# Half of the down products in the summed quarters by seven block products, in equal super-units

## What is computed

```python
x = x + cross_attention(rms_norm(x, g_cross[l]), mem_n, w_cq[l], w_ckv[l], w_co[l])
u = jnp.einsum('bsd,df->bsf', rms_norm(x, g_mlp[l]), w_up[l])
x = x + jnp.einsum('bsf,fd->bsd', jnp.square(jax.nn.relu(u)), w_down[l])
```

## Time and profile before

| what | us |
|---|---|
| median of 3 runs (1203.5 to 1203.62) | 1203.58 |
| the profiled execution's own time | 1203.42 |
| its span | 1201.6 |
| TensorE busy | 1182.1 |
| VectorE busy | 853.1 |
| ScalarE busy | 628.7 |
| POOL busy | 177.8 |

### The profile page before, as it was taken

The page is one execution under the profiler, slowest core; times in us unless marked ns, Lnnn a source line. Parts: engine busy times, 40 slices in busy tenths (PEclk is TensorE's granted clock), DMA queues, the critical chain, the costliest instruction groups (busy, mean ns, idle before and its releaser), DMA issues.

```text
span 1201.6 us, 19272 instructions
## 1 busy us (share of the span) xinstructions
PE 1182.1 (98%) x6776; PEld 1035.6 (86%) x6776; DVE 853.1 (71%) x1149; ACT 628.7 (52%) x927; POOL 177.8 (15%) x177
## 2 busy tenths in 40 slices
PE   9999999999999999999999999999999999999996
PEld 7888899999989889888788888788888888888885
DVE  5758766786668867676887666877767787666554
ACT  6445455555645657555544555544655454555442
POOL 2907400030322404200000000000000000000341
PEclk9999999999999999999999999999999999999999
DMA  9674553443644543456456454547543746555531
GB/s 357 252 260 173 196 175 140 162 154 140 246 162 165 181 159 142 151 198 209 166 176 253 175 181 168 210 149 271 175 176 139 264 157 220 191 182 187 198 140 70
DMA packets 51455, 224.43 MB, mean 187 GB/s; under 512 B 3792, under 2 KB 4176, under 8 KB 31696
## 3 DMA queue, kind: packets, MB, share of 16 engines
q1 hardware_dynamic: 50688, 220.22, 50.8%
q10 hardware_dynamic: 720, 3.59, 0.8%
HBM read 221.69 MB, written 2.10 MB: 186 GB/s over the span
## 4 chain that ended last, share of the span: by engine, by line
PE 93%; DVE 3%; ACT 1%; issue 1%; POOL 1%; DMA 1%; SPq 0%; DVEq 0%; ACTq 0%; POOLq 0%
PE bank L1301 16%; PE bank L1298 16%; PE bank L1299 15%; PE extra L1557 6%; PE extra L1559 5%; PE extra L1558 5%; PE bank L1303 4%; PE bank L1305 4%; PE bank L1304 4%; PE bank L1344 3%; PE bank L1346 3%; PE bank L1345 3%; DVE w_low L813 1%; PE bank L1570 1%; PE bank L1571 1%
## 5 line engine op out<-in xcount | busy, mean ns | idle before, releaser
L813 DVE TENSOR_TENSOR w_low<-staged,w_high 128x1024 fp32r<-128x1024 f32 x311 | 390.0, 1269 | 145.5 <-ACT w_high L433 134.9
L433 ACT ACTIVATE w_high<-staged 128x1024 fp32r<-128x1024 f32 x304 | 314.6, 1053 | 189.8 <-PE bank L1301 81.2
L1299 PEld LDWEIGHTS bank<-part_a,w_low 128*128 128x128 f32 x1408 | 264.6, 188 | 61.4
L1298 PE MATMUL bank<-part_a,w_high 128*128 128x512 f32 x704 | 281.0, 399 | 0.0
L1301 PE MATMUL bank<-part_a,w_high 128*128 128x512 f32 x704 | 278.5, 396 | 0.0
L1299 PE MATMUL bank<-part_a,w_low 128*128 128x256 f32 x1408 | 276.8, 278 | 0.0
L719 ACT ACTIVATE w_high<-staged 128x1024 fp32r<-128x1024 f32 x114 | 118.9, 1058 | 108.9 <-PE extra L1559 92.0
L1133 DVE TENSOR_TENSOR w_low<-staged,w_high 128x1024 fp32r<-128x1024 f32 x114 | 137.4, 1221 | 33.8 <-ACT w_high L719 32.6
L361 POOL TENSOR_TENSOR squares<-x 128x256 f32<-128x256 f32 (+1 forms) x31 | 37.3, 1204 | 685.2 <-DVE x L1257 661.3
L1298 PEld LDWEIGHTS bank<-part_a,w_high 128*128 128x128 f32 x704 | 133.7, 190 | 0.6 <-DVE w_low L813 0.3
L1301 PEld LDWEIGHTS bank<-part_a,w_high 128*128 128x128 f32 x704 | 132.0, 187 | 0.0
(11 more groups left out here) (201 smaller groups left out, 1775.1 us busy)
## 6 DMA issues: line engine op xcount, KB each, us to landing
staged<-in_wup SPq DMA_DIRECT2D x64, 1024.0 KB, 4.8
staged<-in_wdown SPq DMA_DIRECT2D x64, 1024.0 KB, 5.0
staged<-in_wqk SPq DMA_DIRECT2D x32, 1024.0 KB, 4.8
staged<-in_wv SPq DMA_DIRECT2D x12, 1024.0 KB, 5.4
staged<-in_wbc SPq DMA_DIRECT2D x8, 1024.0 KB, 4.8
staged<-in_wmk SPq DMA_DIRECT2D x4, 1024.0 KB, 4.7
staged<-in_woa SPq DMA_DIRECT2D x4, 1024.0 KB, 4.8
staged<-in_wcq SPq DMA_DIRECT2D x4, 1024.0 KB, 4.8
```

The source lines that it names most:

```text
L433: nc.scalar.activation(w_high[:, job % 2, cols], staged[:, job % 4, cols], ACT.Copy).then_inc(high_ready, 1)
L813: tt(w_low[:, job % 2, cols], staged[:, job % 4, cols], f32(w_high[:, job % 2, cols]), ALU.subtract).then_inc(low_ready, 1)
L1298: mm(out[:, :], high, both, start=first, stop=False)
L1299: last = mm(out[:, 0:T], low, part[:, slot(kt), 0, :], start=False, stop=False)
```

## The change

A summed quarter's down product is now four super-units (pairs) of equal form. Pairs 0 and 1 belong to the first 1024 outputs, 2 and 3 to the others. A pair takes one unit by seven products (0 or 2) and one ordinary unit (1 or 3): 42 + 48 matmuls in 11 halves, in the order of three products, half of the ordinary unit, four products, the other half. The products' weights always use slots 0 and 1, the ordinary unit's always 2 and 3. The seven products' sums stay in PSUM over two pairs, and only then four sums of 128x1024 add them to running sums, which are kept apart per PSUM bank in a `y` of twice the size. They are combined once, by twelve VectorE sums in the first eight up jobs of quarter 3; the transposes follow, four behind each of the last eight up jobs. The token sums are made for units 0 and 2, in the first and the third up group. Before the first pair, the split of its first ordinary half comes ahead of the last up tile's arithmetic. The two norm sums move into the first half of the second job. The wait for the cleared `y` moves to the first pair. PSUM is named as two tensors of four banks, and `rope` moves into space that is used again later.

```diff
 SUMMED_QUARTERS = 3
-GROUP_HALVES = 20
-GROUP_STEPS = 12
-QUARTER_HALVES = 2 * QUARTER + 2 * GROUP_HALVES
-FREE_STEPS = 8
-H_SUMS, H_B, H_C = 7, 12, 16
+PAIRS = 4
+PAIR_HALVES = 12
+GROUP_STEPS = 4
+QUARTER_HALVES = 2 * QUARTER + PAIRS * PAIR_HALVES
+FREE_STEPS = 4
+H_B11, H_B21, H_B22, H_R, H_T, H_R_END = 0, 1, 2, 3, 5, 10
+SLOT_S, SLOT_R = 0, 2
...
-        part_s = sb("part_s", [P, 2, 2, 4 * P], F32R)
-        common = sb("common", [P, 2, 512])
+        part_s = sb("part_s", [P, 4, 2, 4 * P], F32R)
+        y_right = sb("y_right", [P, 8, 512])
...
+                    for s, free in enumerate((-2, -2, H_T - PAIR_HALVES, 0)):
+                        sp.wait_ge(low_ready, mlp(q)(2) + (H_MLP + free))
+                        sp.dma_start(staged[:, s, :], wup_in[q * 16 + s, :, :]).then_inc(landed[s], 16)
...
+            def load_down(q):
+                for k in range(PAIRS):
+                    load_unit(q, k, k % 2 * 2, SLOT_S, (-2, -2) if k else (-6, -4))
+                    load_unit(q, k, k % 2 * 2 + 1, SLOT_R, (H_T - PAIR_HALVES, 0) if k else (-2, 0))
...
+            nc.gpsimd.memset(y[0], 0.0).then_inc(y_clear, 1)
+            nc.gpsimd.memset(y[1], 0.0).then_inc(y_clear, 1)
...
             with act.Fori(0, SUMMED_QUARTERS) as q:
-                up_group(q, 0, True)
-                with act.Fori(1, QUARTER // 4 - 1) as i:
-                    up_group(q, i)
+                up_group(q, 0, 0)
+                up_group(q, 1)
+                up_group(q, 2, 2)
                 for s in range(4):
                     if s < 2:
                         split(mlp(q, 3), JOB_MLP + s + 2, 0)
-                    else:
-                        s_tiles(q, 0, (2 * s - 4,))
-                    up(q, 3, s)
-                    if s < 2:
+                        up(q, 3, s)
                         split(mlp(q, 3), JOB_MLP + s + 2, 1)
                     elif s == 2:
-                        s_tiles(q, 0, (1,))
+                        s_tile(q, 0, H_B11)
+                        up(q, 3, s)
+                        s_tile(q, 0, H_B21)
                     else:
-                        r_tiles(q, 0, 3, SLOT_RA[0], 0, (0,))
-                for g in range(2):
-                    r_tiles(q, g, 3, SLOT_RA[g], 2 * g, (1, 2, 3))
-                    s_sums(q, g)
-                    r_tiles(q, g, H_B, SLOT_RB[g], 1 + g, (0, 1, 2, 3)) if g == 0 else r_tiles(
-                        q, g, H_B, SLOT_RB[g], 3, (0, 1, 2, 3))
-                    r_tiles(q, g, H_C, SLOT_RC[g], 1 + 2 * g, (0, 1, 2, 3))
-                    if g == 0:
-                        s_tiles(q, 1, (0, 1, 2))
-                        r_tiles(q, 1, 3, SLOT_RA[1], 2, (0,))
+                        s_tile(q, 0, H_B22)
+                        r_tile(q, 0, 0)
+                        up(q, 3, s)
+                for k in range(PAIRS):
+                    r_tile(q, k, 1)
+                    s_sums(q, k)
+                    r_tile(q, k, 2)
+                    r_tile(q, k, 3)
+                    if k < PAIRS - 1:
+                        for n in (H_B11, H_B21, H_B22):
+                            s_tile(q, k + 1, n)
+                        r_tile(q, k + 1, 0)
...
+            def step(q, k, n):
+                pair = (banks_all, extras_all)[n // 2][:, n % 2 * 2:n % 2 * 2 + 2, :]
+                to = y[k // 2][:, 2 * n:2 * n + 2, :]
+                dve.wait_ge(half_done, down_half(q, k) + (H_T + 1, H_T + 3, H_R_END, PAIR_HALVES)[n])
+                tt(to, to, pair, ALU.add).then_inc(y_step, 1)
+
+            def down_pair(q, k, ahead):
+
+                last = k % 2
+                sum_of_weights(q, k, 1)
+                r_tile(q, k, 1)
+                sum_of_weights(q, k, 2)
+                s_sum(q, k, 0)
+                sum_of_weights(q, k, 3)
+                for n in range(1, 4):
+                    s_sum(q, k, n)
+                r_tile(q, k, 2)
+                if last:
+                    step(q, k, 0)
+                r_tile(q, k, 3)
+                if last:
+                    step(q, k, 1)
                 ahead(0)
+                if last:
+                    step(q, k, 2)
                 ahead(1)
-                step(q, g, 8)
-                step(q, g, 9)
                 ahead(2)
-                step(q, g, 10)
-                step(q, g, 11)
+                if last:
+                    step(q, k, 3)
                 ahead(3)
...
+            def combine(g, n):
...
+                to, one, two = ((y[g][:, 4, :], y[g][:, 4, :], m1), (m6, m6, m1), (m7, m7, m6),
+                                (y[g][:, 6, :], y[g][:, 6, :], m6), (tokens_2, tokens_2, twice(3)),
+                                (right, right, twice(1)))[n]
...
+                tt(to, one, two, ALU.add).then_inc(y_made, 1)
...
+                        r_tile(q, 0, 0)
+                        up(q, 3, s)
+                dve.wait_ge(y_clear, 2)
+                for k in range(PAIRS):
+                    down_pair(q, k, next_pair(q, k + 1) if k < PAIRS - 1 else next_quarter(q))
...
+                    if between is not None and n == count // 2:
+                        norm_sum(between, extra[3])
...
+            def down_pair(q, k):
+                unit, opens, ends = k % 2 * 2, k % 2 == 0, k % 2 == 1
+                steps = q * (2 * GROUP_STEPS) + (FREE_STEPS + k // 2 * GROUP_STEPS)
+                if k == 0:
                     pe.wait_ge(taken, mlp(q)(1) + (BANKS + OUT_MLP + 13))
-                pe.wait_ge(hid_low, q * 16 + (1 + 4))
-                pe.wait_ge(y_step, steps - 4)
-                s_half(q, g, 0, bank[0], block_of(0, 0), ends=True)
-                pe.wait_ge(y_step, steps - 3)
-                s_half(q, g, 1, extra[0], block_of(1, 0))
-                pe.wait_ge(y_step, steps - 1)
-                pe.wait_ge(s_low, q * 2 + 2)
-                s_half(q, g, 2, extra[1], sum_of(3))
-                pe.wait_ge(y_step, steps)
-                for n in range(4):
-                    r_half(q, g, 3, n, 1)
-                if g == 0:
+                pe.wait_ge(hid_low, q * 16 + (1 + 4 * unit + 4))
+                if opens:
+                    pe.wait_ge(y_step, steps - 3)
+                s_half(q, k, H_B11, bank[0], block_of(unit, 0, 0), opens, ends)
+                if opens:
+                    pe.wait_ge(y_step, steps - 1)
+                s_half(q, k, H_B21, extra[0], block_of(unit, 1, 0), opens)
+                if opens:
+                    pe.wait_ge(y_step, steps)
+                pe.wait_ge(s_low, q * 4 + (unit + 2))
+                s_half(q, k, H_B22, extra[2], sum_of(unit, 3), opens)
+                r_half(q, k, 0)
+                r_half(q, k, 1)
+                if k == 0:
                     pe.wait_ge(taken, mlp(q)(1) + (BANKS + OUT_MLP + 16))
-                s_half(q, g, H_SUMS, bank[1], sum_of(0), ends=True)
-                s_half(q, g, H_SUMS + 1, bank[3], sum_of(2), ends=True)
-                s_half(q, g, H_SUMS + 2, bank[2], sum_of(1), ends=True)
-                s_half(q, g, H_SUMS + 3, extra[2], block_of(1, 1), opens=False, done_by=2)
-                for n in range(4):
-                    r_half(q, g, H_B, n, 2)
-                for n in range(4):
-                    r_half(q, g, H_C, n, 3)
+                s_half(q, k, H_T, bank[1], sum_of(unit, 0), opens, ends)
+                s_half(q, k, H_T + 1, bank[3], sum_of(unit, 2), opens, ends)
+                s_half(q, k, H_T + 2, bank[2], sum_of(unit, 1), opens, ends)
+                s_half(q, k, H_T + 3, extra[1], block_of(unit, 1, 1), ends=ends, done_by=2)
+                r_half(q, k, 2)
+                r_half(q, k, 3)
...
+            for n in range(KT // 2):
                 up(3, n // 4, n % 4)
-                if n == 0:
-                    pe.wait_ge(y_step, SUMMED_QUARTERS * 2 * GROUP_STEPS + FREE_STEPS)
+            for n in range(KT // 2):
+                up(3, 2 + n // 4, n % 4)
+                g = n // 4
+                if n % 4 == 0:
+                    pe.wait_ge(y_made, 6 * g + 6)
                 if n >= 4:
                     pe.wait_ge(y_added, n - 3)
-                for t in range(QT):
-                    last = nc.tensor.transpose(extra[n % 4][:, t * P:(t + 1) * P],
-                                               y[:, t, n * P:(n + 1) * P], ident)
+                for tile in range(2 * n, 2 * n + 2):
+                    for t in range(QT):
+                        last = nc.tensor.transpose(
+                            extra[n % 4][:, tile % 2 * T + t * P:tile % 2 * T + (t + 1) * P],
+                            y[g][:, 4 + 2 * (tile % 8 // 4) + t, tile % 4 * P:(tile % 4 + 1) * P], ident)
                 last.then_inc(y_turned, 1)
```

More of the change, by code:

```diff
@@ L307, in _, with load_up @@
             stream(wco_in, JOB_CO, CROSS)
-            def load_up(q):
-                with sp.Fori(0, QUARTER // 4) as i:
+            def load_up(q, first):
+                if first:
+                    for s in range(4):
```

(36 more changed lines are left out.)

293 lines of the change are left out of this document (121 added, 172 removed).

## The result

The changed kernel takes 1213.26 us (median of 4 runs, 1212.03 to 1213.92), the kernel before 1203.54 in the same comparison: a ratio of 1.0078, 95% interval 1.0064 to 1.0093. It is slower by 9.7 us. Forecast were 1210.0, within 1198 to 1215; the measured time lies 3.3 us above the first and 0.3 above the likeliest case's own range (1206 to 1213). The profiled execution took 1212.03 us with a span of 1210.2.

What follows compares the result with a forecast made beforehand. TensorE, busy 98% of the span, was taken to bound the kernel, with VectorE and the load queue next. 1203.4 - 8.2 - 3.3 - 2.0 - 0.6 + 20.7 = 1210.0 us, range 1198 to 1215.

Steps and rivals of the forecast that it cites:

- likeliest case: Whole kernel: gets slower, products saved on TensorE being paid by VectorE and loads released late; 1206 to 1213 us, chance 0.48.
- TensorE's work: Down stage: 186 matmuls per group become 180, so 36 fewer over six groups at 0.2267 us, -8.2 us.
- The entry: Start of three quarters' down stages: splitting the first ordinary half earlier removes TensorE's 1.1 us wait each, -3.3 us.
- the entry term of the other side: Entering a quarter's first pair: VectorE needs six operations (6.9 us) to the second sum product, +0.6 us a quarter.
- The norm sums: Two norm sums moved 1.39 us later: TensorE's waits of 0.9 and 1.1 us for POOL go, -2.0 us.
- Quarter 3: Up jobs of quarter 3: 16 places with two transposes become 8 with four, eight changes of kind fewer, -0.6 us.
- The two loops: Down stage: VectorE's order and late-released loads make TensorE wait 6.9 us per quarter, three quarters, +20.7 us.
- exit: Leaving a quarter's last pair: the next up weights land at 16.71 us, due at 16.42, +0.3 us per quarter.
- TensorE's work did not decide: Rival: loads and VectorE keep ahead, so all of the 20.7 us stays away: 1189.3 us, chance 0.12.
- loop B: Second to third pair, running sums taken out: seven VectorE steps after the first block lands delay TensorE, +3.0 us per quarter.
- the rival with queued loads 2.95 us apart: Load queue at 355 GB/s: third load comes 0.6 us later at six boundaries, 1213.5 us; chance 0.05.
- Late first loads: Rival: first loads land late, as one burst's 5.8 us, each boundary paying in full: to 1220 us, chance 0.05.

Runs made afterwards that it cites:

- before_orders: Kernel before with only the norm sums in the second job and a quarter's first ordinary half split ahead of the last up tile's arithmetic: 1199.41 us, ratio 0.9962.
- without the differences: Changed kernel with the four differences of weight blocks per pair left out on VectorE, products taking the plain blocks: 1200.53 us, ratio 0.9975.
- half of the bytes: Changed kernel loading only half of each block's columns for the seven products, all waits and engine work kept: 1200.57 us, ratio 0.9973.
- released row by row: Changed kernel with each chunk of blocks loaded in two 512 KB halves, each issued when its own block's last low part is made: 1201.11 us, ratio 0.9977.
- a running sum in the gap: Changed kernel with the third running sum taken before the next pair's first low part, while VectorE waits for the load: 1212.37 us, ratio 1.0072.
- the three relieved kernels: Changed kernel without weight-block differences (1200.53 us), with half of the blocks' bytes loaded (1200.57 us), or with blocks' loads issued per row (1201.11 us).

## Why the prediction was right, point by point

**TensorE's work, -8.2 us.** 36 matmuls went at 0.2267 us each. That they are worth it is inferred from the account: no run isolates them.

**The entry, -3.3 us.** The wait of 1.06 us (distance of starts: 1.2) is gone in the trace, with the late starts behind it 4.1 us in all, so this term was too small. Undone alone it cost 1.4 to 2.4 us, 1.5 by the traces. The difference is the entry term of the other side, which the prediction held separately (+0.6 a quarter): the two are one trade. In the kernel before, less was paid for it: the down stage's lateness fell from 4.6 us to 1.5 with both reorderings and the moved wait, and what is left is mostly a new wait of 0.2 to 0.3 us before each quarter's second ordinary half. Together they brought 5.4 us against 2.4 + 3.6.

**The norm sums, -2.0 us.** -2.4 by the milestones, 2.1 to 3.0 by undoing (1.9 to 2.1 by the start of the down stage). The prediction named the end of VectorE's wait for the clearing only as a bonus. It was a condition: without it (`before_orders`) the time is 1.3 us longer and the down stage starts 0.9 us later than with it.

**Quarter 3, -0.6 us.** This term was wrong: nothing was gained. A job with four transposes takes 6.03 us, one with two took 5.80, one with none 5.57, so four add 0.46 us, twice the 0.23 of two, and not the 0.36 of the forecast. The sixteen up jobs of quarter 3 take 92.69 us where they took 92.68. (The last stretch of the account is 0.4 us better than the two before it because quarter 2's down stage waits less: 7.65 us, after 7.9 and 8.0.) The combination cost nothing: the first eight jobs keep 5.57.

**The two loops, +20.7 us.** The mechanism was right and its size slightly low. A quarter of 178.8 us holds 360 x 0.2267 = 81.6 us of down matmuls and 89.2 us of up jobs (16, 5.57 apart), so 8.0 us of waits, where 6.9 were predicted; before, 175.0 less 84.3 and 89.2 is 1.5 us, where 1.1 were counted. Queued loads land 2.7 us apart, not 2.66; besides, each wait makes the next few starts late by some 0.1 to 0.2 us, which the prediction left out. Against 20.7 us, the down stages' lateness is 23.5. In us over the three quarters, by place:

| kernel | entry | first to second pair | second to third | third to fourth | exit |
|---|---|---|---|---|---|
| predicted | 1.8 | 4.5 | 9.0 | 4.5 | 0.9 |
| the kernel before | 4.1 | 0.2 | 0.3 | 0.1 | 0.0 |
| changed | 2.5 | 5.8 | 9.2 | 5.2 | 0.9 |
| changed, again | 2.4 | 5.9 | 9.1 | 5.2 | 2.8 |
| without the differences | 0.0 | 3.9 | 4.4 | 3.1 | 1.2 |
| half of the bytes | 2.5 | 0.6 | 5.5 | 0.2 | 2.8 |
| released row by row | 2.5 | 1.0 | 5.5 | 0.8 | 1.5 |
| without the running sums | 2.5 | 6.2 | 5.1 | 5.3 | 1.4 |
| a running sum in the gap | 2.4 | 5.7 | 7.1 | 5.2 | 2.5 |
| ordinary half behind the up tile | 4.0 | 6.3 | 9.2 | 5.0 | 2.0 |

The boundary with the running sums came out as forecast, 9.2 us against 9.0; the two plain ones have 11.0 against 9.0, part of it as a wait before the pair's first product; and the entry 2.5 against 1.8. The exit has 0.9 here, as forecast, and 2.8 in the second profile of the same kernel: there the first up load lands up to 6.3 us after its issue, where the prediction took 5.0. That agreement is partly luck, and why the load takes longer behind quarters 0 and 1 was not found.

The sum with measured terms: -8.2 for the matmuls, -4.6 for the waits of the old down stages, +23.5 for those of the new, -2.4 for the norm sums, 0.0 for quarter 3, and +0.2 for the up jobs of quarters 1 and 2 (89.3 us each, 89.2 before): +8.5 us, against +8.6 measured. Forecast were +6.6. The errors partly cancel: the loops, quarter 3 and the up jobs were 3.6 us too low in all, the entry and the norm sums gave 1.7 more than they were put at. The median lies another 1.2 us above the profiled execution, which was the fastest of the four.

**The rivals.** TensorE's work did not decide. Even the three relieved kernels came to 1200.5 to 1201.1 us and not to the 1189 of that rival: once one member of the chain is relieved, loop B's own VectorE steps, the exit and, but for the kernel without differences, the entry stay. That the queue's rate alone decides was excluded by the loads released row by row. The measured median is next to the 1213.5 of the rival with queued loads 2.95 us apart, but not for its reason: they landed 2.71 and 2.73 us apart. Late first loads, as the other rival has them, were seen at the exits, and within a quarter only at quarter 1's first boundary (5.4 us, issued at 762.7). The Trainium skill's limit of about 358 GB/s (DMA: Bandwidth & Descriptors, "Where 436 GB/s comes from") would put queued loads 2.93 us apart, an estimate from that page. The 2.71 and 2.73 us between ScalarE's starts do not agree with it; they are 387 and 384 GB/s. The page gets its limit by halving a memory stack's 716 GB/s between two cores; this program runs on one, and no run here loads from a second.

**Left open.** The order of the ordinary unit's load ahead of the blocks' was not tried by itself, nor another place for the running sums than the one shown.

## What to carry to other kernels

Work saved on the engine that bounds a kernel is only worth the slack of those that feed it, and slack must be read in order, not on average: VectorE was to be busy 38.6 of 40.8 us, and the pairs still waited, because a buffer was given back only at the end of a gapless run of eight steps and its load's 5 us and the splits came behind that. Write down one turn of the loop (last use of the buffer, issue, landing, first use) and compare it with the bounding engine's turn; then release each part of a buffer at its own last use. And when a change brings several moves, try the cheap ones alone: here they were the gain.

## What the hardware showed that was not expected

Three loads of 1 MB issued 0.4 and 0.55 us apart in one queue landed 5.1, 7.4 and 9.6 us after their issue, so 2.7 us behind one another. The first load of the up weights behind a down stage took between 4.7 and 6.5 us to land, and in a kernel that waits for it this alone moved the time by 1.9 us between two executions. (That the changed kernel spreads more from run to run than the one before is not shown: four and five runs within 1.9 and 1.5 us, against 21 of the kernel before within 1.8.) Two 128x128 transposes between jobs cost 0.23 us and four 0.46, so putting them together saved nothing. And a mean or a busy share of TensorE can hide waits: 36 matmuls less and 0.6 us more "busy".
